# A transformer block with a product-key expert layer on one core: weights of v made for two chunks at a time, row dots written in place, h laid out in blocks of 32 tokens

## The chip, the cores and the metric

The kernel runs on one core of a Trainium2 chip. The metric is device time in microseconds of one execution of the whole program; lower is better. Engines are named as in the profile: PE (TensorE matmuls), PEld (its weight loads), DVE (VectorE), ACT (ScalarE), POOL (GpSimd), SP (SyncE, here a queue of DMA issues).

## What is computed

One block over 512 tokens of width 1024, in float32: adaptive norm, three kinds of attention, a projection, and a feed-forward layer of experts chosen by product keys. The change lies in the last part:

```python
def chunk(xc):                                   # xc: tokens x 1024
    q = einsum('td,de->te', xc, wq)              # 8 heads x 2 halves x 128
    s = einsum('thpd,hpnd->thpn', q, sub_keys)   # 128 key scores per half
    sv, si = top_k(s, 16)
    ...                                          # the best 16 of the 256 sums per head
    g = softmax(top)                             # gates of the 8 x 16 chosen experts
    a = gelu(einsum('thkd,td->thk', u[eidx], xc))
    return einsum('thk,thkd->td', g * a, v[eidx])
```

## The kernel before

The 16384 experts are 128 chunks of 128. Tokens 0 to 127 (tile 0) are done by gathering: for each of 128 choices two rows of 1024 per token are fetched by indirect DMA (from u and from v), a dot of the u row with h goes to a gelu, and the v row is added with that weight to `y0`. Tokens 128 to 511 are done densely: for each chunk all gelus are computed (`a_chunk`: u times h, 128 experts x 384 tokens) and multiplied by a table of gates that is zero for experts not chosen, and the result is the weight of a matmul with v (`v_chunk`).

Each float32 matmul is made of three passes on split operands: x_hi is x rounded to the matmul's type (ACT writes it), x_lo is the rest (DVE subtracts). So a chunk of u, of v, and of the weights w each need a hi and a lo, and h has both from the start (`h_hi`, `h_lo`, written once by `take_h2T` on ACT and `h_low` on DVE, from PSUM).

Stages, in order of time:

1. The mixer, to about 310 us.
2. Queries and key scores (`q_passes`, 24 matmuls for each of 16 pieces, moving operand h with all 512 tokens), to about 406 us.
3. Chunks 0 to 64 of `a_chunk`, 24 matmuls of 384 columns each, with the making of the gates table between them, to 768 us. Gelus of the first 56 chunks are stored to DRAM (`spill`).
4. The joint loop, to about 1290 us: step m does `v_chunk(m)` (18 matmuls of 512 columns) and then `a_chunk(m + 65)`.
5. v chunks alone, to about 1556 us; from m = 72 the gelus come back from DRAM, four chunks to a load (L1096), beside the gates (`g_in`, L1092).

Work is ordered by hand in each engine's program, with semaphores between engines. In step m of stages 4 and 5 DVE runs `chunk(m)`: `weigh(m)` (gelus times gates to `w_f`, a copy to `w_hi`, the rest to `w_lo`), `split_v(m)` (v_lo), one or two row dots with `row_sum`s, and u_lo for chunk m + 65. ACT runs `parts(m)`: v_hi of m + 1, the small gelus of the row dots, u_hi, and the gelu of `a_chunk(m + 64)`. `v_hi` and `v_lo` have two places, so ACT may write v_hi(m) only when `v_chunk(m - 2)` is done (semaphore `v_product_done`). `weigh` waits for that too, before its copy:

```python
dve.tensor_tensor(w_f..., a_act[:, c, :]..., g_in[:, (c // 4) % 2, :, c % 4, :], ALU.mult).then_inc(s_pw, 1)
dve.wait_ge(s_pw, i + 1)
if not end:
    after(dve, s_yv, i - 1)
dve.tensor_copy(hi[:, q, :], w_f[:, :]).then_inc(s_whi, 1)
dve.wait_ge(s_whi, i + 1)
dve.tensor_tensor(lo[:, q, :], w_f[:, :], hi[:, q, :].bitcast(f32), ALU.subtract)
```

`load_g` on SP loads gates (and from chunk 72 on gelus) of four chunks into one of two places, when the chunks that used the place are done. The last four chunks (`at_end`) have buffers of their own, so that PE can finish one output tile after the other.

## Time and profile before

| | us |
|---|---|
| device time, median of 3 runs | 1568.46 (1567.51 to 1569.08) |
| span of the profiled execution, first to last instruction | 1565.4 |
| PE busy (share of the span) | 1527.4 (98%) |
| DVE busy | 1337.7 (85%) |
| ACT busy | 660.1 (42%) |
| POOL busy | 487.5 (31%) |

The span leaves out what lies before the first and behind the last instruction, so it is 2.1 us under the lowest run and 3.1 us under the median. Matmuls overlap in the records: one is listed with some 0.39 us (512 columns), but the next begins 0.227 us after it. What a matmul costs is read from the distance between starts, and whether PE waits is read from gaps in that distance.

### The profile page before, as it was taken

The numbers are of one execution on the slowest core, as the hardware profiler recorded it, in microseconds if no ns is written. First come the engines' busy times: TensorE is split into PE (matmuls) and PEld (weight loads), VectorE is DVE, ScalarE is ACT, GpSimd is POOL, SyncE is SP. The second block draws the span as 40 slices with busy tenths as digits, with TensorE's granted clock in tenths as the row PEclk, the third lists the DMA queues.
The fourth block names the chain that finished last, engine by engine and source line by source line (L and its number), as shares of the span: only waits on it lengthen the run. The fifth ranks groups of instructions, "written<-read, shape, count | busy, mean of one in ns | idle before, by whom it ended". The sixth has DMA issues, their size and how long they took to land.

```text
span 1565.4 us, 24588 instructions
## 1 busy us (share of the span) xinstructions
PE 1527.4 (98%) x8275; PEld 1363.9 (87%) x8275; DVE 1337.7 (85%) x2877; ACT 660.1 (42%) x1143; POOL 487.5 (31%) x450
## 2 busy tenths in 40 slices
PE   4999999999999999999999999999999999999997
PEld 4887767888999999999999999999999998888886
DVE  5788666549999989899698898899999998999977
ACT  3444554233344757657433333343333332333232
POOL 1121300033450000020355455456566663233000
PEclk9999999999999999999999999999999999999999
DMA  9754410132355565676899999999999999999772
GB/s 366 270 174 148 148 68 0 55 95 82 118 169 180 194 230 199 229 248 251 298 393 330 350 340 343 346 337 371 372 378 372 368 345 355 376 350 352 241 244 104
DMA packets 160467, 398.77 MB, mean 255 GB/s; under 512 B 11753, under 2 KB 75369, under 8 KB 158705
## 3 DMA queue, kind: packets, MB, share of 16 engines
q1 hardware_dynamic: 112992, 227.06, 41.7%
q0 software_dynamic: 36864, 134.23, 23.2%
q10 hardware_dynamic: 10514, 36.30, 5.9%
q8 instruction: 47, 0.77, 0.2%
q14 instruction: 50, 0.41, 0.1%
HBM read 359.27 MB, written 38.27 MB: 254 GB/s over the span
## 4 chain that ended last, share of the span: by engine, by line
PE 83%; DVE 13%; DMA 1%; ACT 1%; issue 1%; ACTq 0%; DVEq 0%; SPq 0%
PE bank_S L907 16%; PE bank_T L907 11%; PE bank_O L858 6%; PE bank_O L856 6%; PE bank_O L857 6%; PE bank_T L885 5%; PE bank_G L907 5%; PE bank_S L856 3%; PE bank_S L857 3%; PE bank_S L858 3%; PE bank_O L643 2%; PE bank_S L610 2%; DVE mod_acc L1909 1%; DVE v_sb L1902 1%; DVE v_sb L1915 1%; DVE si L1921 1%
## 5 line engine op out<-in xcount | busy, mean ns | idle before, releaser
L1462 ACT ACTIVATE v_hi<-v_raw 128x1024 fp32r<-128x1024 f32 x124 | 131.7, 1062 | 333.9 <-PE bank_G L907 330.9
L1434 ACT ACTIVATE u_hi<-u_raw 128x1024 fp32r<-128x1024 f32 x128 | 135.9, 1061 | 243.0 <-PE bank_O L858 122.8
L1213 POOL COPY stage<-eidx 128x1 uint32<-128x1 uint32 (+1 forms) x128 | 75.7, 591 | 461.8 <-DVE eidx L2030 207.7
L1217 POOL DMA_INDIRECT row<-in_peer_u,stage x128 | 148.1, 1157 | 103.8 <-POOL stage L1213 103.8
L856 PE MATMUL bank_S<-h_hi,u_hi 128*128 128x384 f32 x512 | 179.7, 351 | 0.5 <-DVE u_lo L2002 0.5
L858 PE MATMUL bank_O<-h_hi,u_lo 128*128 128x384 f32 x512 | 171.9, 336 | 0.0
L856 PE MATMUL bank_O<-h_hi,u_hi 128*128 128x384 f32 x512 | 171.7, 335 | 0.0
L858 PE MATMUL bank_S<-h_hi,u_lo 128*128 128x384 f32 x512 | 171.5, 335 | 0.0
L857 PE MATMUL bank_O<-h_lo,u_hi 128*128 128x384 f32 x512 | 171.5, 335 | 0.0
L857 PE MATMUL bank_S<-h_lo,u_hi 128*128 128x384 f32 x512 | 171.4, 335 | 0.0
L2098 DVE SCALAR_TENSOR_TENSOR y<-row,wgt,y 128x1024 f32<-128x1024 f32 x128 | 165.9, 1296 | 0.0
L2108 DVE TENSOR_TENSOR v_lo<-v_raw,v_hi 128x1024 fp32r<-128x1024 f32 x124 | 152.0, 1226 | 12.1 <-ACT v_hi L1462 0.6
L2121 DVE SCALAR_TENSOR_TENSOR junk<-row,h 128x1024 f32<-128x1024 f32 x128 | 155.8, 1217 | 0.0
L1217 POOL DMA_INDIRECT row<-in_peer_v,stage x128 | 141.6, 1106 | 41.9 <-issue 30.3
L907 PE MATMUL bank_S<-v_hi,w_lo 128*128 128x512 f32 x372 | 125.4, 391 | 0.0
L907 PE MATMUL bank_S<-v_lo,w_hi 128*128 128x512 f32 x372 | 125.3, 391 | 0.0
L907 PE MATMUL bank_S<-v_hi,w_hi 128*128 128x512 f32 x372 | 125.2, 391 | 0.0
L1505 ACT ACTIVATE g_out<-bank_T 128x512 f32<-128x512 f32 x96 | 104.7, 1122 | 46.6 <-PE bank_T L885 38.2
L2057 DVE TENSOR_SCALAR hot_i<-iota_k,cols 128x128 f32<-128x128 f32 x384 | 106.6, 341 | 1.0 <-PE bank_T L885 0.2
L885 PE MATMUL bank_T<-hot_i,hot_j 128*128 128x128 f32 x768 | 101.8, 275 | 1.2 <-DVE hot_j L2059 1.2
L885 PEld LDWEIGHTS bank_T<-hot_i,hot_j 128*128 128x128 f32 x768 | 97.6, 191 | 3.6 <-issue 2.1
L856 PEld LDWEIGHTS bank_O<-h_hi,u_hi 128*128 128x128 f32 x512 | 96.1, 188 | 2.5
(370 smaller groups left out, 3647.8 us busy)
## 6 DMA issues: line engine op xcount, KB each, us to landing
u_raw<-in_u_t SPq DMA_DIRECT2D x128, 512.0 KB
v_raw<-in_peer_v SPq DMA_DIRECT2D x128, 512.0 KB
gates<-g_out ACTq DMA_DIRECT2D x12, 2048.0 KB, 6.8
g_in<-gates SPq DMA_DIRECT2D x32, 768.0 KB
ada_late<-in_w_ada SPq DMA_DIRECT2D x8, 2048.0 KB, 8.4
spill<-a_act ACTq DMA_DIRECT2D x56, 192.0 KB, 2.1
a_act<-spill SPq DMA_DIRECT2D x14, 768.0 KB, 10.6
w_raw<-in_w_in SPq DMA_DIRECT2D x20, 512.0 KB, 4.1
```

Of the source, the lines that this page charges most:

```text
L856: pe.matmul(ps[:, 0:DT], u_hi[q][:, kk], h_hi[:, GT:NT, k, :], start=(k == 0), stop=False)
L857: pe.matmul(ps[:, 0:DT], u_hi[q][:, kk], h_lo[:, GT:NT, k, :], start=False, stop=False)
L858: mm = pe.matmul(ps[:, 0:DT], u_lo[q][:, kk], h_hi[:, GT:NT, k, :], start=False, stop=(k == KD - 1))
L885: mm = pe.matmul(ps[:, tok * P:tok * P + P], hot_j[:, b % 2, tok, :], hot_i[:, b % 2, tok, :], start=True, stop=True)
L907: mm = pe.matmul(y_bank[t][half][:, :], w[:, q, tt], v[:, q, half * 512:half * 512 + 512], start=(first and n == 0), stop=False)
L1217: pool.indirect_dma_start(rows[slot][:, :], None, table[:, :], bass.IndirectOffsetOnAxis(stage[:, place:place + 1], 0))\
L1434: act.activation(u_hi[c % 2][:, :], u_raw[:, c % 2, :], ACT.Copy).then_inc(s_uhi, 1)
L1462: act.activation(v_hi_end[:, i % TAIL, :] if end else v_hi[:, c % 2, :], v_raw[c % 4][:, :], ACT.Copy)\
L2057: dve.tensor_scalar(hot_i[:, B % 2, tok, :], iota_k[:, :], cols[:, 0, n:n + 1], cols[:, 2, n:n + 1], ALU.is_equal, ALU.mult)
L2098: dve.scalar_tensor_tensor(out=y0[:, :], in0=rows[2 * place + 1][:, :], scalar=wgt[:, q], in1=y0[:, :], op0=ALU.mult, op1=ALU.add).then_in ...
L2108: dve.tensor_tensor(lo[:, q, :], v_raw[c % 4][:, :], hi[:, q, :].bitcast(f32), ALU.subtract)\
L2121: dve.scalar_tensor_tensor(out=junk[:, :], in0=rows[2 * place][:, :], scalar=1.0, in1=h2[:, 0, :], op0=ALU.mult, op1=ALU.mult, accum_out=d ...
```

## The change

- **Weights in pairs.** `weigh` is gone. On DVE `product` multiplies gelus by gates for two chunks in one instruction and writes the result over the gates in `g_in`; ACT's new `w_high` makes w_hi of both chunks; DVE's `w_low` makes w_lo of both. In step m, DVE does `w_low` of the pair (m, m + 1) if m is even and `product` of the pair (m + 1, m + 2) if m is odd, in front of `split_v(m)`. ACT does `w_high` of the pair (m + 2, m + 3) at the end of `parts(m)`, m even. `w_hi` and `w_lo` have two places of a pair each. PE waits for the pair's count.
- **Loads of gates** now wait for w_lo of the pairs that used the place, where they waited for the products.
- **Row dots** write their full-length product over the gathered u row, where they wrote to `junk`.
- **h in blocks.** `h_hi` and `h_lo` are stored as 16 blocks of 32 tokens (block, then the 8 pieces of the width, then the token), where there were 4 tiles of 128. The moving operand of each matmul of `a_chunk` is then 12 runs of 32 columns, 256 values (1024 bytes) apart, where it was 3 runs of 128; in `q_passes` 16 runs instead of 4.
- **Places.** Several buffers move in memory; `u_lo1` now lies over tile 0 of `h_lo`, for which POOL waits once for the last query.

```diff
-        h_hi = at("h_hi", 32, [P, NT, KD, P], f32r)
-        h_lo = at("h_lo", 64, [P, NT, KD, P], f32r)
+        h_hi = at("h_hi", 32, [P, S // GB, KD, GB], f32r)
+        h_lo = at("h_lo", 64, [P, S // GB, KD, GB], f32r)
...
+        def gate_pair(c):
+
+            return g_in[c // 4 % 2][:, :, c % 4:c % 4 + 2, :].rearrange("p b i t -> p i b t")
+
+        def by_block(pair):
+            return pair.rearrange("p i (b t) -> p i b t", t=GB)
...
-                    pe.matmul(ps[:, 0:DT], u_hi[q][:, kk], h_hi[:, GT:NT, k, :], start=(k == 0), stop=False)
+                    pe.matmul(ps[:, 0:DT], u_hi[q][:, kk], h_hi[:, GT * P // GB:S // GB, k, :], start=(k == 0), stop=False)
...
-                pe.wait_ge(s_w, i + 1)
+                pe.wait_ge(s_w, over(i, c, 2) + 1)
                 pe.wait_ge(s_vlo, i + 1)
...
-                    after(sp, s_pw, 4 * (q - 1))
+                    after(sp, s_w, 2 * (q - 1))
...
+                if i == 1:
+                    taken(pool, ("q", 2 * PH - 1))
...
-                act.activation(h_hi[:, i, 4 * half:4 * half + 4, :], ps, ACT.Copy).then_inc(s_hhi, 1)
+                act.activation(half_columns(h_hi, i, half), ps.rearrange("p a (n t) -> p a n t", t=GB), ACT.Copy)                   .then_inc(s_hhi, 1)
...
+            def w_high(i, c):
+
+                if not within(i):
+                    return
+                if at_end(i):
+                    act.wait_ge(s_acc, PH * TOPK)
+                else:
+                    after(act, s_yv, i - 2)
+                act.wait_ge(s_pw, over(i, c, 2) + 1)
+                act.activation(weight_pair(w_hi, w_hi_end, i, c), gate_pair(c), ACT.Copy).then_inc(s_whi, 1)
...
             act.wait_ge(s_gst[1], 16 * (BLOCKS // 2))
+            w_high(0, 0)
+
...
+                if c % 2 == 0:
+                    w_high(m + 2, c + 2)
...
+            def product(i, c):
+
+                if not within(i):
+                    return
+                late = isinstance(i, int) and i >= MAIN
+                dve.wait_ge(s_g[c // 4 % 2], 16 * (over(i, c, 8) + 1))
                 if late:
-                    dve.wait_ge(s_al[c // 4], 2 * (i - c) - 2 * MAIN + 16)
+                    dve.wait_ge(s_al[c // 4 % 2], 16 * ((i - MAIN) // AHEAD + 1))
                 else:
-                    dve.wait_ge(s_gelu, i + SPILL + 1)
...
+                    dve.wait_ge(s_gelu, i + SPILL + 2)
+                slot = c % AHEAD
+                dve.tensor_tensor(gate_pair(c), by_block(a_act[:, slot:slot + 2, :]), gate_pair(c), ALU.mult)\
+                   .then_inc(s_pw, 1)
+
+            def w_low(i, c):
+
+                dve.wait_ge(s_whi, over(i, c, 2) + 1)
+                if not at_end(i):
+                    after(dve, s_yv, i - 2)
+                dve.tensor_tensor(weight_pair(w_lo, w_lo_end, i, c), gate_pair(c),
+                                  weight_pair(w_hi, w_hi_end, i, c).bitcast(f32), ALU.subtract).then_inc(s_w, 1)
...
-                weigh(i, c, late)
+                if c % 2 == 0:
+                    w_low(i, c)
+                else:
+                    product(i + 1, c + 1)
...
-                    dve.scalar_tensor_tensor(out=junk[:, :], in0=rows[2 * place][:, :], scalar=1.0, in1=h2[:, 0, :],
+                    dve.scalar_tensor_tensor(out=rows[2 * place][:, :], in0=rows[2 * place][:, :], scalar=1.0,
+                                             in1=h2[:, 0, :],
...
+            product(0, 0)
             chunk_loop(dve, chunk_and_tile)
```

DVE at the entry of the joint loop, before: v_lo of chunk 0, then the three instructions of `weigh(0)`, the first row dot, u_lo of chunk 65, `weigh(1)` and v_lo of chunk 1.

```order
L2108 TENSOR_TENSOR v_lo<-v_raw_132,v_hi 128x1024 [waits gates_stored0,v_hi_ready,gates_made,vector_steps]
L2076 TENSOR_TENSOR w_f<-a_act,g_in 128x384 [waits gelu_done,gates_loaded0,gates_stored1]
L2085 CAST w_hi<-w_f 128x384 [waits w_product]
L2087 TENSOR_TENSOR w_lo<-w_f,w_hi 128x384 [waits w_hi]
L2121 SCALAR_TENSOR_TENSOR junk,dots<-row_150,h_107 128x1024 [waits row_got0,w_ready]
L2131 TENSOR_TENSOR u_lo_140<-u_raw,u_hi_138 128x1024 [waits u_hi_ready]
```

The same place with the change: the product (`g_in<-a_act,g_in`) and w_lo of the pair, between which DVE waits for ACT (`waits w_hi`), and in step 1 the product of the next pair in front of v_lo of chunk 1.

```order
L2142 TENSOR_TENSOR v_lo<-v_raw_133,v_hi 128x1024 [waits gates_stored0,v_hi_ready,gates_made,vector_steps]
L2114 TENSOR_TENSOR g_in_130<-a_act,g_in_130 128x2x12x32 [waits gelu_done,gates_loaded0,gates_stored1]
L2122 TENSOR_TENSOR w_lo_150<-g_in_130,w_hi_148 128x768 [waits w_hi]
L2158 SCALAR_TENSOR_TENSOR row_152,dots<-row_152,h_107 128x1024 [waits row_got0]
L2169 TENSOR_TENSOR u_lo_141<-u_raw,u_hi_139 128x1024 [waits u_hi_ready]
L2114 TENSOR_TENSOR g_in_130<-a_act,g_in_130 128x2x12x32 [waits gelu_done,gates_loaded0]
L2142 TENSOR_TENSOR v_lo<-v_raw_134,v_hi 128x1024 [waits v_hi_ready]
```

What moved: the making of w_hi has left DVE, and the first v chunk now waits for a chain over DVE, ACT and DVE again. ACT at the same place with the change, from v_hi of chunk 0 to v_hi of chunk 2:

```order
L1482 ACTIVATE v_hi<-v_raw_133 128x1024 [waits v_loaded0,gates_stored0]
L1454 ACTIVATE u_hi_139<-u_raw 128x1024 [waits u_loaded1,a_done]
L1502 ACTIVATE a_act<-bank_S 128x384 [waits a_done,gelus_stored1]
L1494 ACTIVATE w_hi_148<-g_in_130 128x768 [waits w_product,gates_stored1]
L1482 ACTIVATE v_hi<-v_raw_134 128x1024 [waits v_loaded1]
L1562 ACTIVATE act_g<-dots 128x1 [waits row_dots]
L1565 ACTIVATE wgt<-act_g,gate 128x1 [waits row_gelus]
L1454 ACTIVATE u_hi_138<-u_raw 128x1024 [waits u_loaded0,a_done]
L1502 ACTIVATE a_act<-bank_O 128x384 [waits a_done,w_product]
L1494 ACTIVATE w_hi_149<-g_in_130 128x768 [waits w_product]
L1482 ACTIVATE v_hi<-v_raw_135 128x1024 [waits v_loaded2,v_product_done]
```

The two `w_hi` rows are new; v_hi of chunks 1 and 2 now stand behind them. DVE in stage 5, steps 118 to 120, before:

```order
L2108 TENSOR_TENSOR v_lo<-v_raw_134,v_hi 128x1024 [waits v_hi_ready,w_ready]
L2141 TENSOR_SCALAR ss<-ss 128x1 [waits x2_squares]
L2076 TENSOR_TENSOR w_f<-a_act,g_in 128x384 [waits gelus_loaded1,gates_loaded1]
L2085 CAST w_hi<-w_f 128x384 [waits v_product_done,w_product]
L2087 TENSOR_TENSOR w_lo<-w_f,w_hi 128x384 [waits w_hi]
L2108 TENSOR_TENSOR v_lo<-v_raw_135,v_hi 128x1024 [waits v_hi_ready,w_ready]
L2076 TENSOR_TENSOR w_f<-a_act,g_in 128x384 [waits gelus_loaded0,gates_loaded0]
```

And with the change:

```order
L2142 TENSOR_TENSOR v_lo<-v_raw_135,v_hi 128x1024 [waits v_hi_ready]
L2179 TENSOR_SCALAR ss<-ss 128x1 [waits x2_squares]
L2114 TENSOR_TENSOR g_in_130<-a_act,g_in_130 128x2x12x32 [waits gelus_loaded0,gates_loaded0]
L2142 TENSOR_TENSOR v_lo<-v_raw_136,v_hi 128x1024 [waits v_hi_ready]
L2122 TENSOR_TENSOR w_lo_150<-g_in_130,w_hi_148 128x768 [waits v_product_done,w_hi]
L2142 TENSOR_TENSOR v_lo<-v_raw_133,v_hi 128x1024 [waits v_hi_ready]
```

The instruction that waits for the loads of chunks 120 to 123 (`gelus_loaded0`, `gates_loaded0`) stood behind v_lo of chunk 119 and now stands in front of it.

## Rows read from the trace of the kernel before

**Rows 1.** The page: busy time of the engines, and the chain that ended last.

```profile
PE 1527.4 (98%) x8275; PEld 1363.9 (87%) x8275; DVE 1337.7 (85%) x2877; ACT 660.1 (42%) x1143; POOL 487.5 (31%) x450
...
PE 83%; DVE 13%; DMA 1%; ACT 1%; issue 1%; ACTq 0%; DVEq 0%; SPq 0%
```

**Rows 2.** Windows: PE, PEld, DVE, ACT, POOL busy (count), granted clock, DMA share, GB/s.

```profile
1080.00:1120.00 40.00, 40.00 (x205) 36.44 (x204) 38.23 (x51) 15.54 (x33) 25.34 (x26) 1.00 0.99 364
...
1360.00:1400.00 40.00, 40.00 (x178) 33.15 (x177) 37.00 (x56) 12.56 (x20) 12.36 (x15) 1.00 1.01 358
```

**Rows 3.** Timeline of PE in the joint loop: start, duration, what; two steps' first matmuls.

```profile
792.82 0.63 PE L907 MATMUL bank_S<-v_hi,w_hi 128*128 128x512 f32 x2
...
801.12 0.63 PE L907 MATMUL bank_S<-v_hi,w_hi 128*128 128x512 f32 x2
```

**Rows 4.** Timeline of PE: 18 matmuls of `q_passes`, and one v chunk of stage 5.

```profile
330.90 0.39 PE L811 MATMUL bank_S<-h_hi,wq_hi 128*128 128x512 f32 x1
...
334.98 0.60 PE L797 MATMUL bank_T<-keys,qT 128*128 128x128 f32 x4
...
1515.65 0.62 PE L907 MATMUL bank_S<-v_hi,w_hi 128*128 128x512 f32 x2
...
1519.73 0.62 PE L907 MATMUL bank_S<-v_hi,w_hi 128*128 128x512 f32 x2
```

**Rows 5.** Timeline of PE: the last a chunk of stage 3, and the first v chunk.

```profile
763.74 0.33 PE L856 MATMUL bank_O<-h_hi,u_hi 128*128 128x384 f32 x1
...
767.89 0.63 PE L907 MATMUL bank_S<-v_hi,w_hi 128*128 128x512 f32 x2
```

**Rows 6.** Groups by line and form: count, busy us, mean ns, idle before and its releasers.

```profile
L2098 DVE SCALAR_TENSOR_TENSOR y<-row,wgt,y 128x1024 f32<-128x1024 f32 x128 | 165.9, 1296 | 0.0
L2108 DVE TENSOR_TENSOR v_lo<-v_raw,v_hi 128x1024 fp32r<-128x1024 f32 x124 | 152.0, 1226 | 12.1 <-ACT v_hi L1462 0.6 <-DVE w_lo L2087 0.3
...
L1434 ACT ACTIVATE u_hi<-u_raw 128x1024 fp32r<-128x1024 f32 x128 | 135.9, 1061 | 243.0 <-PE bank_O L858 122.8 <-PE bank_S L858 79.3 <-DMA u_raw<-in_u_t 18.2
...
L1505 ACT ACTIVATE g_out<-bank_T 128x512 f32<-128x512 f32 x96 | 104.7, 1122 | 46.6 <-PE bank_T L885 38.2 <-ACT a_act L1471 8.4
...
L2076 DVE TENSOR_TENSOR w_f<-a_act,g_in 128x384 f32<-128x384 f32 x128 | 70.4, 550 | 1.1 <-ACT a_act L1471 1.0
L2087 DVE TENSOR_TENSOR w_lo<-w_f,w_hi 128x384 fp32r<-128x384 f32 x124 | 69.4, 559 | 4.3
...
L2085 DVE CAST w_hi<-w_f 128x384 fp32r<-128x384 f32 x124 | 45.2, 365 | 47.5 <-PE bank_G L907 40.4 <-DVE w_f L2076 0.4
...
L1471 ACT ACTIVATE a_act<-bank_O 128x384 f32<-128x384 f32 x64 | 30.3, 474 | 4.7 <-PE bank_O L858 4.7
```

**Rows 7.** Waits: who waited for whom, us in total, times, longest.

```profile
ACT v_hi L1462 <- PE bank_G L907: 330.9, 121, 3.6
```

**Rows 8.** Timeline at the entry of the joint loop, POOL and DVE.

```profile
765.42 0.18 POOL L1213 COPY stage<-eidx 128x1 uint32<-128x1 uint32 x1 [70.47 <-DMA g_in<-gates]
...
765.45 0.57 DVE L2076 TENSOR_TENSOR w_f<-a_act,g_in 128x384 f32<-128x384 f32 x1 [1.02 <-ACT a_act L1471]
...
766.44 0.56 DVE L2087 TENSOR_TENSOR w_lo<-w_f,w_hi 128x384 fp32r<-128x384 f32 x1
```

**Rows 9.** Loads of gelus from DRAM (L1096), one of their issues, and v_lo of chunk 119.

```profile
DMA to landing us min/median/max: 7.9/10.6/12.0
...
1502.80 0.75 SPq L1096 DMA_DIRECT2D a_act<-spill  x1
...
1517.02 1.23 DVE L2108 TENSOR_TENSOR v_lo<-v_raw,v_hi 128x1024 fp32r<-128x1024 f32 x1
```

**Rows 10.** Timelines of DVE and PE: where h_lo and the last v_lo are ready and used.

```profile
313.67 0.69 DVE L1800 TENSOR_TENSOR h_lo<-bank_T,h_hi 128x512 fp32r<-128x512 f32 x1 [0.29 <-ACT h_hi L1360]
...
316.72 0.47 PE L811 MATMUL bank_S<-h_hi,wq_hi 128*128 128x512 f32 x1
...
1544.22 1.23 DVE L2108 TENSOR_TENSOR v_lo_end<-v_raw,v_hi_end 128x1024 fp32r<-128x1024 f32 x1
...
1546.93 0.39 PE L916 MATMUL bank_S<-v_hi_end,w_hi_end 128*128 128x512 f32 x1
```

68 lines of the change are left out of this document (29 added, 39 removed).

## The prediction

> **What bounds the kernel now.** I read the page first, for who is busy and whose work ends last: PE is busy 98% of the span and 83% of the last-ending chain is PE; DVE has 13% of it [rows 1]. A busy PE in this profile is not yet a PE without gaps, since records overlap, so the second view is the windows of the stages that the change touches. In the joint loop PE is busy all of 40 us, DVE 38.23 of 40; in the v stage PE all of 40, DVE 37.00. The granted clock is 1.00 in both, its 2.4 GHz level, and the DMA engines are full, 0.99 and 1.01 [rows 2]. Third, distances between starts, to see whether PE waits anywhere. A step of the joint loop takes 801.12 - 792.82 = 8.30 us [rows 3]. Alone, its parts take 767.89 - 763.74 = 4.15 us (24 matmuls of 384 columns) [rows 5] and 1519.73 - 1515.65 = 4.08 us (18 of 512) [rows 4], 8.23 in sum. So at most 0.07 us of a step is anything but matmuls, and nothing can be won there but those 63 x 0.07 = 4.4 us. Fourth, the waits: ACT waits 330.9 us for the end of v chunks, 121 times, before it may write the next v_hi [rows 7]. That is the signature of a bound PE: the makers of operands are early and are held back by PE's use of the buffers. The reader should keep two questions apart: how much DVE work goes away (much), and whether PE ever waited for it (no).
>
> **Part 1, weights in pairs: the work.** A DVE subtraction takes 1226 ns for 1024 elements and 559 for 384 [rows 6], 1.04 ns an element, so 768 take 559 + 384 x 1.04 = 0.96 us. Before, a pair of chunks cost 2 x (0.550 + 0.365 + 0.559) = 2.95 us on DVE; with the change 0.96 (product) + 0.96 (w_low) = 1.92. DVE loses 1.03 us a pair, 66 us over 64 pairs. The product reads gates in runs of 32 already in `w_f` (0.550 us, no dearer than w_lo's 0.559), so the pair's pattern adds nothing. ACT gains 64 copies of 768: between its copies of 384 (0.474) and 1024 (1.061) lies 0.83 us [rows 6]; 53 us in all on an engine busy for 660 [rows 1]. All of it is hidden, because PE does not wait for DVE or ACT in either loop. Worth on the end: 0. If DVE had been what PE waits for, 66 us would be at stake; the 0.07 us of a step say that it isn't.
>
> **Part 2, the entry of the loop: the one place with a price.** Before, the gates land at 765.42 (POOL is released by them), DVE's `w_f` starts at 765.45, and w_lo is ready at 766.44 + 0.56 = 767.00 [rows 8]; PE ends its last a chunk at 767.89 and goes on without a gap [rows 5]. Slack 0.89 us. Now the product ends at 765.45 + 0.96 = 766.41, w_high at 766.46 + 0.83 = 767.29, w_low at 767.34 + 0.96 = 768.30 (0.05 us for each passing from engine to engine, the order of the 0.03 us between landing and `w_f` in these rows). PE starts `v_chunk(0)` at 768.35: **+0.45 us**. By the bounds of w_high (0.80, proportional to u_hi's 1061 ns, to 1.06, all of it) it is 0.4 to 0.7. Behind the wait on ACT stands v_hi of chunk 1, now done at 768.4; its v_lo is needed 8.3 us after the loop's start. On DVE the first dot and u_lo of chunk 65 stand behind w_low: ready at 768.3 + 1.3 + 1.2 = 770.8 (by the instructions of their length in [rows 6]), needed at 768.35 + 4.1 = 772.4. Nothing further is late.
>
> **Part 3, inside the loops.** ACT's w_high(m + 2) waits for the product that DVE makes at the start of step m + 1, and v_hi(m + 2) stands behind it. But v_hi(m + 2) waits for `v_chunk(m)` anyway, and DVE, tied to v_hi(m + 1), is in step m + 1 before that. Cost 0. On DVE the product of chunks 4q and 4q + 1 now stands ahead of v_lo(4q - 1), and it waits for loads. Take chunk 120: its gelus are issued at 1502.80; the product could start after v_lo(118), about 1514.1 (one 4.08 step before the end of v_lo(119), 1518.2); the slowest of the 14 loads took 12.0 us, landing at 1514.8; v_lo(119) starts at 1517.02 in any case, held by PE [rows 9]. PE needs v_lo(119) at 1519.73 [rows 4], so it stays unharmed up to a landing at 1519.73 - 1.23 - 0.96 - 0.1 = 1517.4, 14.6 us after the issue. Margin 2.6 us over the worst. Cost 0.
>
> **Part 4, the tail, the dots, the new wait of POOL.** The last v_lo is ready at 1544.22 + 1.23 = 1545.45 and used at 1546.93 [rows 10]; DVE is lighter there than before, so it is not later. Cost 0. The dot writes to another address; if in place it took what the dearest instruction of its length takes, 1.296 us [rows 6], 128 of them still fit into DVE's slack and what it just lost. POOL's new wait is for the last query, which ACT's u_hi(1), already awaited, stands behind. Cost 0.
>
> **Part 5, h in blocks.** The evictions: 8 copies by ACT and 8 subtractions by DVE, now written in runs of 32. No row has a write in such runs by ACT; its nearest are contiguous ones (0.59 for 512, between 0.474 and 1.061) and `g_out`'s, scattered by single elements, 1.122 [rows 6]. Runs of 32 are nearer to contiguous: 0. The upper bound, +0.53 twice behind the last tile, would still meet 316.72 - 314.36 = 2.4 us of slack at the first matmul that reads it [rows 10]; it could hold up the other copies there by 0.5 us. The matmuls: 1 run (v, 512 columns) and 4 runs (`q_passes`, 512 columns, 334.98 - 330.90 = 4.08 us for 18) cost the same, 226.7 ns each [rows 4], and 3 runs cost 4.15/24 = 172.9 [rows 5]. Taking columns off at 2.4 GHz leaves 13.3, 13.3 and 12.9 ns. Runs therefore cost nothing that can be seen: at the 0.01 us of these rows, under 0.2 ns for each run more. I take 0. Upper bound: 9 runs more x 0.2 x 3120 matmuls (24 in each of 128 chunks, and 48 of the first queries, on three tiles) plus 12 x 0.2 x 336 (the other 14 queries) = 6.4 us. Below zero is excluded, since one run is no cheaper than four.
>
> Beside these rows, the Trainium skill (TensorE: Matmul & The Clock Gate, on 56 ns instead of 53.3) states a fixed cost of some 2.5 ns per warm matmul over N / 2.4 GHz. The rows differ, 13 ns, and they decide. If the 10.5 ns between were the price of how the moving operand is read, new runs could change 3120 matmuls by up to 33 us, an estimate from that page; that the contiguous v pays the same speaks against it. And SBUF — State Buffer (on cachelines) says that reads are at full rate while hits on a 16-byte line are consecutive, which runs of 32 floats keep: by that rule the block form costs 0 as well, where the bound above is 6.4; no row here has PE reading runs this short.
>
> **The sum.** On the profiled execution's own time, span 1565.4: +0.45 = 1565.85 us. The median of the runs is 3.1 us over that span; so **1568.9 us**, in effect no change. A change under 0.2% (3.1 us) can't be told from none by such runs.
>
> **Rivals.**
> 1. *Short runs slow the matmuls* (slower). If each run more costs one cycle of the 2.4 GHz clock, 0.42 ns, it is 9 x 0.42 x 3120 + 12 x 0.42 x 336 = 13.5 us: 1582.4. It decides from 0.9 ns a matmul on (3.1 us / 3456). For it: no row has such runs. Against it: 1, 3 and 4 runs cost alike. Chance 0.12.
> 2. *DVE waits for loads ahead of v_lo* in the v stage (slower). Each of 14 loads would pay what it lands later than 14.6 us after its issue; 1 us each makes 1582.9. Against it: the slowest took 12.0. With other small losses, chance 0.05.
> 3. *The 0.07 us of a step come from DVE and ACT beside PE*, and a lighter DVE gives them back (faster): up to 4.4 us, 1564.5. Against it: ACT gets more to do at just these moments. Chance 0.09.
> 4. *DVE or its buffers hold PE somewhere that I don't see*, so that part of the 66 us is real (faster); 5 to 10 us, some 1561. Against it: the steps' arithmetic. Chance 0.06.
> 5. *The pairing saves DVE nothing*, since the long patterns run slower: then DVE is as busy as now, and PE still doesn't wait: 1568.9, in with the forecast.
>
> **The numbers.** Forecast with rival 5: 0.68, its own range 1566 to 1572. Faster 0.15 (3 and 4), slower 0.17 (1 and 2). The range takes in most of rival 3, the upper bound of 6.4 us and half of rival 1: 1563.5 to 1576. Left out: the far ends of 1, 2 and 4, some 0.14.
>
> **What the profile after should show.** A step of the joint loop still 8.30 us, a v chunk 4.08, both to 0.01; a matmul of 384 columns in stage 3 at 173 ns and `q_passes` at 226.7 (rival 1: 176 to 177 and more). DVE busy near 1272, ACT near 713. The first v chunk at about 768.3, with a gap of 0.45 us before it. The product 0.96 us, w_high 0.83. v_hi still waiting for PE some 300 us. Any distance of v chunks over 4.08 in the v stage, once in four, is rival 2; a step under 8.27 is rival 3. I would be wrong above all if the distance of matmuls depends on the layout of h.

## The result: 11 us slower

| | before | with the change |
|---|---|---|
| device time, median | 1568.77 us (1567.51 to 1570.10, 4 runs) | 1580.07 us (1579.26 to 1580.31, 4 runs) |
| span of the profiled execution | 1565.4 us | 1578.5 us |

The ratio is 1.0073, with a 95% interval of 1.0059 to 1.0087. The forecast was 1568.9 us with a range up to 1576. The time lies above that range, on the side of rival 1. The medians are 11.3 us apart. The two profiled executions, from which all that follows is read, are the fastest of the four before and the slowest of the four after, 12.8 us apart and 13.1 in span; a sum by stages therefore comes out somewhat above 11.3.

The page of the changed kernel, busy times and the chain that ended last, against [rows 1]:

```profile
PE 1541.2 (98%) x8275; PEld 1377.0 (87%) x8275; DVE 1273.5 (81%) x2621; ACT 706.3 (45%) x1207; POOL 544.1 (34%) x450
...
PE 95%; DVE 3%; DMA 1%; ACT 1%; issue 0%; SPq 0%; DVEq 0%; ACTq 0%
```

DVE is lighter by 64.2 us and ACT heavier by 46.2, near what was forecast. But PE, with the same 8275 matmuls, is busy for 13.8 us more, and the span is 13.1 longer. An engine that does the same instructions in more busy time has not waited: its instructions have become slower.

Windows in the joint loop and in the v stage (columns as in [rows 2]):

```profile
1090.00:1130.00 40.00, 40.00 (x204) 36.69 (x203) 35.64 (x40) 17.20 (x35) 27.20 (x26) 1.00 0.99 369
1370.00:1410.00 40.00, 40.00 (x178) 33.11 (x178) 31.93 (x36) 16.01 (x25) 19.28 (x16) 1.00 1.00 352
```

The granted clock is 1.00, the 2.4 GHz level, as before, so the clock is not the reason. Next the distances. PE's timeline, the starts of two steps of the joint loop, against [rows 3]:

```profile
793.93 0.63 PE L924 MATMUL bank_S<-v_hi,w_hi 128*128 128x512 f32 x2
...
802.30 0.63 PE L924 MATMUL bank_S<-v_hi,w_hi 128*128 128x512 f32 x2
```

A step takes 8.37 us; it took 8.30. The same timeline in `q_passes` (18 matmuls from the first row to the second) and, behind them, one v chunk of stage 5, against [rows 4]:

```profile
331.00 0.40 PE L829 MATMUL bank_S<-h_lo,wq_hi 128*128 128x512 f32 x1
...
335.26 0.40 PE L829 MATMUL bank_S<-h_lo,wq_hi 128*128 128x512 f32 x1
...
1520.56 0.62 PE L924 MATMUL bank_S<-v_hi,w_hi 128*128 128x512 f32 x2
...
1524.64 0.62 PE L924 MATMUL bank_S<-v_hi,w_hi 128*128 128x512 f32 x2
```

The v chunk still takes 4.08 us, although its weights are now made in pairs. 18 matmuls of the queries, which the pairs don't touch, take 4.26 instead of 4.08. The third place is the last a chunk of stage 3 and the first v chunk, against [rows 5]:

```profile
772.67 0.34 PE L873 MATMUL bank_O<-h_hi,u_hi 128*128 128x384 f32 x1
...
776.76 0.34 PE L875 MATMUL bank_O<-h_hi,u_lo 128*128 128x384 f32 x1
777.11 0.70 PE L924 MATMUL bank_S<-v_hi,w_hi 128*128 128x512 f32 x2
```

Here the last matmul starts 4.09 us after the chunk's first, 23 distances of 178 ns, and then 0.35 us pass instead of 0.18: a gap of 0.17. The groups by form say the same of all chunks. The row of before, of one of the three passes of an a chunk:

```profile
L857 PE MATMUL bank_O<-h_lo,u_hi 128*128 128x384 f32 x512 | 171.5, 335 | 0.0
```

and of the changed kernel:

```profile
L874 PE MATMUL bank_O<-h_lo,u_hi 128*128 128x384 f32 x512 | 174.1, 340 | 0.0
```

PE does not stand idle in front of either ("0.0" in both rows). The whole loss, by stage, from the starts of all matmuls in the two traces:

| | before | with the change | difference |
|---|---|---|---|
| up to the first query | 302.52 | 303.14 | +0.62 |
| queries, to the first a chunk | 104.04 | 107.37 | +3.33 |
| stage 3, to the first v chunk | 361.33 | 366.59 | +5.26 |
| joint loop | 523.14 | 527.02 | +3.88 |
| v alone | 265.19 | 265.17 | -0.02 |
| mean distance, queries (512 columns) | 230.9 ns | 240.2 ns | +9.3 |
| mean distance, a chunks of stage 3 (384) | 173.4 ns | 177.8 ns | +4.4 |

The distances of the queries are those of the steady part, and those of stage 3 of its first 80 us. The mean of a query includes its first distance, 314 ns before and 321 with the change; most of the others are 227 before and 233 to 240 now. The loss sits wherever PE reads h, and nowhere else. Summed over every matmul of a kind, the distances close the account: queries +3.32 us (384 matmuls), a chunks of stage 3 +5.63 (1560, on average +3.6 ns, since later in the stage some were dearer already), the gates' matmuls among them -0.37, a chunks of the joint loop +4.83 (1511 distances, +3.2 ns), v chunks of the joint loop -0.95 (1134). That is 12.46 us, the three stages' 12.47. The rest of the 13.1 is the 0.62 ahead of the first query, which lies in front of everything changed.

The rest of the changed kernel's profile. Groups by form of what was new or moved:

```profile
L2142 DVE TENSOR_TENSOR v_lo<-v_raw,v_hi 128x1024 fp32r<-128x1024 f32 x124 | 151.9, 1225 | 119.0 <-ACT v_hi L1482 118.9
...
L2114 DVE TENSOR_TENSOR g_in<-a_act,g_in 128x768 f32<-128x768 f32 x64 | 60.9, 951 | 2.6 <-DMA a_act<-spill 1.9 <-DMA g_in<-gates 0.7
...
L2122 DVE TENSOR_TENSOR w_lo<-g_in,w_hi 128x768 fp32r<-128x768 f32 x62 | 58.9, 951 | 1.0 <-ACT w_hi L1494 1.0
...
L1494 ACT ACTIVATE w_hi<-g_in 128x768 fp32r<-128x768 f32 x62 | 51.7, 834 | 1.9 <-DVE g_in L2114 1.9
```

The waits of the pair that makes v's parts, the first against [rows 7]:

```profile
ACT v_hi L1482 <- PE bank_G L924: 286.8, 122, 3.6
...
DVE v_lo L2142 <- ACT v_hi L1482: 118.9, 116, 5.1
```

v_lo now stands idle for v_hi 118.9 us in all (0.6 in [rows 6]), and v_hi stands idle for PE. Not all of this is new: before, DVE waited for PE in front of its copy to w_hi (47.5 us of idle time in [rows 6]), and that wait has moved to v_lo. Over the whole span DVE's idle time, span less busy time, grew from 227.7 to 305.0 us: 64.2 of freed work and 13.1 of longer span. So the saving became idle time and went no further.

### The profile page after: what moved, and what is told of

Its sections match the earlier page's. It is cut to its first block, busy times and chain, and to the rows that moved or that the text cites. A ratio compares the mean times of both kernels' runs of the same rounds, so it can differ in the third digit from the quotient of the medians.

```text
span 1578.5 us, 24179 instructions
## 1 busy us (share of the span) xinstructions
PE 1541.2 (98%) x8275; PEld 1377.0 (87%) x8275; DVE 1273.5 (81%) x2621; ACT 706.3 (45%) x1207; POOL 544.1 (34%) x450
## 4 chain that ended last, share of the span: by engine, by line
PE 95%; DVE 3%; DMA 1%; ACT 1%; issue 0%; SPq 0%; DVEq 0%; ACTq 0%
PE bank_S L924 16%; PE bank_T L924 11%; PE bank_O L873 6%; PE bank_O L875 6%; PE bank_O L874 6%; PE bank_S L873 6%; PE bank_S L875 6%; PE bank_S L874 6%; PE bank_T L902 5%; PE bank_G L924 5%; PE bank_S L830 2%; PE bank_S L828 2%; PE bank_S L829 2%; PE bank_O L659 2%; PE bank_S L626 2%; PE bank_T L639 1%
## 5 line engine op out<-in xcount | busy, mean ns | idle before, releaser
L2142 DVE TENSOR_TENSOR v_lo<-v_raw,v_hi 128x1024 fp32r<-128x1024 f32 x124 | 151.9, 1225 | 119.0 <-ACT v_hi L1482 118.9
L1233 POOL COPY stage<-eidx 128x1 uint32<-128x1 uint32 (+1 forms) x128 | 98.8, 772 | 414.1 <-DVE eidx L2064 209.9
L1237 POOL DMA_INDIRECT row<-in_peer_u,stage x128 | 159.0, 1242 | 104.1 <-POOL stage L1233 103.0
L873 PE MATMUL bank_S<-h_hi,u_hi 128*128 128x384 f32 x512 | 183.0, 357 | 0.0
L1237 POOL DMA_INDIRECT row<-in_peer_v,stage x128 | 164.5, 1285 | 41.9 <-issue 41.3
L875 PE MATMUL bank_S<-h_hi,u_lo 128*128 128x384 f32 x512 | 174.8, 341 | 0.0
L875 PE MATMUL bank_O<-h_hi,u_lo 128*128 128x384 f32 x512 | 174.4, 341 | 0.0
L2158 DVE SCALAR_TENSOR_TENSOR row<-row,h 128x1024 f32<-128x1024 f32 x128 | 156.6, 1224 | 0.0
L874 PEld LDWEIGHTS bank_O<-h_lo,u_hi 128*128 128x128 f32 x512 | 96.5, 188 | 2.5
```

The source lines that it names most:

```text
L873: pe.matmul(ps[:, 0:DT], u_hi[q][:, kk], h_hi[:, GT * P // GB:S // GB, k, :], start=(k == 0), stop=False)
L874: pe.matmul(ps[:, 0:DT], u_hi[q][:, kk], h_lo[:, GT * P // GB:S // GB, k, :], start=False, stop=False)
L875: mm = pe.matmul(ps[:, 0:DT], u_lo[q][:, kk], h_hi[:, GT * P // GB:S // GB, k, :], start=False, stop=(k == KD - 1))
L1237: pool.indirect_dma_start(rows[slot][:, :], None, table[:, :], bass.IndirectOffsetOnAxis(stage[:, place:place + 1], 0))\
L2142: dve.tensor_tensor(lo[:, q, :], v_raw[c % 4][:, :], hi[:, q, :].bitcast(f32), ALU.subtract)\
L2158: dve.scalar_tensor_tensor(out=rows[2 * place][:, :], in0=rows[2 * place][:, :], scalar=1.0, in1=h2[:, 0, :], op0=ALU.mult, op1=ALU.mult, ...
```

## The experiments

### First: undo the block form, or do it alone

`e1_pairs_tiles128` is the changed kernel with h in tiles of 128 again:

```diff
-        h_hi = at("h_hi", 32, [P, S // GB, KD, GB], f32r)
-        h_lo = at("h_lo", 64, [P, S // GB, KD, GB], f32r)
+        h_hi = at("h_hi", 32, [P, S // HB, KD, HB], f32r)      # HB = 128
+        h_lo = at("h_lo", 64, [P, S // HB, KD, HB], f32r)
```

> The changed kernel with h stored again in 4 tiles of 128 tokens; pairs, dots in place and all places in memory stay as changed. Theory R (the price is the short runs of the moving operand): the median falls back to that of the kernel before plus the entry gap of the joint loop, less what the changed kernel won in its joint loop (v matmuls there 228.2 ns against 229.1): 1566 to 1569 us, a matmul of 384 columns at 173 ns and of q_passes at 227 to 231 in the mean. Rival P (the pairs or the new places, u_lo over the old h_lo tile, cost it): it stays at 1578 to 1580 with 177 to 178 ns.

Measured: 1569.03 us (11 runs) against 1568.11, ratio 1.0006 (0.9997 to 1.0015). Its distances are those of before: queries 230.8, a chunks 173.4 ns.

`e2_before_blocks32` is the kernel before with that one edit the other way, h in blocks of 32 (HB = 32), and nothing of pairs, dots or places:

> The kernel before with h alone in blocks of 32 tokens, nothing else changed. Theory R: 11 to 15 us over the kernel before (q_passes +3.2 us, the other a matmuls 3072 x 4.4 ns = 13.5 us), 1580 to 1584 us; a matmul of 384 columns at 177 to 178 ns. Rival P: no change, 1568 to 1569 us, 173 ns.

Measured: 1579.82 us (5 runs), ratio 1.0075 (1.0061 to 1.0089). Queries 107.37 us, stage 3 366.70, joint loop 526.92, v alone 265.17, distances 240.2 and 177.8 ns: each the number of the changed kernel. PE's line on its page, 12.6 us more busy than before's, though DVE (1342.4) is as heavy as before:

```profile
PE 1540.0 (98%) x8275; PEld 1375.5 (87%) x8275; DVE 1342.4 (85%) x2877; ACT 659.3 (42%) x1143; POOL 479.3 (30%) x450
```

Undone, the edit takes the loss away; alone, it brings all of it. That settles which part of the change was slow. What it is in a block of 32 that costs is another question.

`e3_before_blocks64` is the same with HB = 64:

> The kernel before with h alone in blocks of 64 tokens (6 runs of 64 for a chunk, 8 for a query). Theory R with a price for each run (about 0.5 ns): +1.5 ns a matmul, 4 to 6 us over the kernel before, 1573 to 1575 us. Rival T (a threshold: runs of 64 or more are free, shorter ones are not): 1568 to 1569 us, 173 ns. Rival T2 (any jump beyond one in 128 columns costs all of it): as with blocks of 32, 1580 us or more.

Measured: 1567.79 us (10 runs), ratio 0.9998 (0.9988 to 1.0007); distances 230.8 and 173.4 ns. Twice the runs of before cost nothing that can be seen, four times the runs cost 11.7 us. A price for each run, theory R, does not give that.

`e4_forms` is the kernel before; its first 64 a chunks read 384 columns of h in six ways in turn (other columns than the right ones in all but the 3 runs of 128, so other numbers are computed):

```diff
+                form = FORMS[i % len(FORMS)] if early else 3      # FORMS = (1, 3, 6, 12, 24, 40)
...
+                    elif form == 12:
+                        pe.matmul(ps[:, 0:DT], u_hi[q][:, kk], h_flat[:, :].rearrange("p (n a t) -> p n a t", n=12, a=KD)[:, :, k, :], start=(k == 0), stop=False)
...
+                    elif form == 40:
+                        pe.matmul(ps[:, 0:DT], u_hi[q][:, kk], h_flat[:, 360 * k:360 * k + 480].rearrange("p (n t) -> p n t", t=40)[:, :, 0:32], start=(k == 0), stop=False)
```

> The kernel before, but the first 64 a chunks read their 384 moving columns in six forms in turn, from the same 12 KB of h: 1 run of 384, 3 of 128 (as before), 6 of 64, 12 of 32, 24 of 16 (all with the spacing that fills the region), and 12 runs of 32 spaced 160 bytes instead of 1024. But for the form of 3 the columns are not those of the right tokens and width, so the gelus of these chunks are of other numbers. Distances between matmuls: theory R, linear in the runs: 172.5, 173.4, 175, 178, 184 ns, and the close spacing like the wide one, 178. Rival T: 173, 173, 173, 178, 178 or more. Rival S (the spacing of 1024 bytes, a power of two, is what costs): 12 runs of 160 bytes spacing at 173, others by their spacing.

Its groups by line in stage 3; the lines are the third pass of 6 runs of 64 (L867), 12 of 32 at 1024 bytes (L871), 24 of 16 at 512 (L875) and 12 of 32 at 160 (L879):

```profile
L867 PE MATMUL bank_S<-h_hi,u_lo 128*128 128x384 f32 x88 | 29.5, 335 | 0.0
...
L871 PE MATMUL bank_S<-h_hi,u_lo 128*128 128x384 f32 x84 | 28.7, 341 | 0.0
...
L875 PE MATMUL bank_S<-h_hi,u_lo 128*128 128x384 f32 x80 | 27.4, 343 | 0.0
...
L879 PE MATMUL bank_S<-h_hi,u_lo 128*128 128x384 f32 x80 | 26.9, 337 | 0.0
```

Median distances: one run of 384 columns 174, 3 and 6 runs 173, 12 runs at 1024 bytes 178, 24 runs 181, but 12 runs at 160 bytes 174. The same number of runs of the same length is dear or cheap by where the runs lie. R and the threshold at a length, T, fell here; the spacing, S, was left, and a new one, C.

### Second: spacing and length, and the pairs once more

The next kernels use one frame: nine forms take the first 64 a chunks in turn, each on lines of its own. A form is given by the columns in a run, the values of 4 bytes from run to run, and a third number. In the two kernels of this part the third is how many values the start moves from one piece k of the width to the next; in the two of the third part it is the first value, the same for all k, and the forms count from the start of tile 0 instead of tile 1. The first form is always h as in the kernel before.

```diff
+FORMS = [(128, 0, 0), (32, 40, 320), (32, 64, 320), (32, 96, 256), (32, 128, 192), (32, 192, 96), (32, 248, 8), (32, 250, 8), (32, 256, 0)]
...
+                    h, l = (spaced(x, k, *FORMS[form]) for x in (h_hi, h_lo))
```

> The kernel before. Of the first 64 chunks of u times h, each of nine forms of the moving operand takes every ninth: 3 runs of 128 as before, then 12 runs of 32 columns with the starts of the runs 160, 256, 384, 512, 768, 992, 1000 and 1024 bytes apart (the columns are not the right ones in these eight forms, so other numbers are computed there; 384 columns are multiplied in each). What is read is the distance between the starts of two matmuls, by form. Known so far: 3 runs of 128 173 ns, 12 of 32 at 160 bytes 174, at 1024 bytes 177 to 179. Theory C (a jump costs PE reading time, more for a far jump, and about 13 ns of each matmul, its distance less 384 columns at 2.4 GHz, cover it): the distance rises smoothly with the spacing, 173 to 174 up to 256 bytes, about 175 to 176 at 512 and 768 bytes, 177 to 178 at 992, 1000 and 1024 alike. Theory S (spacing by a power of two is what costs): 1024 bytes 177 to 178, 512 bytes perhaps too, and 992, 1000, 768 and 384 near 173 to 174. Theory T (the length of the run decides, whatever the spacing): all eight at 177 to 178 but 160 bytes, which would be the odd one; it has nearly fallen already.

> The kernel before. Of the first 64 chunks of u times h, each of nine forms of the moving operand takes every ninth: 3 runs of 128 as before, then 4 runs of 96 (3072 bytes apart), 6 of 64 (2048), 8 of 48 (1536), 16 of 24 (768), 16 of 24 (128 bytes apart), 24 of 16 (512), 24 of 16 (96 bytes apart), 48 of 8 (256); the columns are the right ones but in the two close forms, 16 of 24 at 128 bytes and 24 of 16 at 96, and all multiply 384. Read: distance between starts. Theory C (n jumps of about 1.45 ns of reading, less for a near jump, are hidden up to about 13 ns a matmul): 4, 6 and 8 runs 173 ns, 16 runs of 24 about 180 to 183, 24 of 16 at 512 bytes 181 to 182 (known), the close forms only 174 to 177, and 48 of 8 over 190. Theory R' (each run over three costs, in proportion): 4 runs 173.5, 6 runs 175, 8 runs 176, 16 runs 180: 6 and 8 runs tell it from C. Theory T (a run under 64 columns costs a fixed sum a matmul): 8 of 48 stands at 177 to 178 already, with 16 of 24 beside it.

One thing in the second text is wrong: in all its forms but the first the columns are not the right ones. All multiply 384 all the same. These two ran once, as did `e4_forms` and the two kernels of the third part, and only their distances are used.

The third pass in the first of the two, spacings of 1000 bytes (L899), 512 (L887), 256 (L879), 160 (L875), 384 (L883) and 992 (L895):

```profile
L899 PE MATMUL bank_S<-h_hi,u_lo 128*128 128x384 f32 x56 | 19.7, 352 | 0.0
...
L887 PE MATMUL bank_S<-h_hi,u_lo 128*128 128x384 f32 x56 | 19.2, 343 | 0.0
...
L879 PE MATMUL bank_S<-h_hi,u_lo 128*128 128x384 f32 x56 | 19.2, 342 | 0.0
...
L875 PE MATMUL bank_S<-h_hi,u_lo 128*128 128x384 f32 x56 | 18.8, 336 | 0.0
...
L883 PE MATMUL bank_S<-h_hi,u_lo 128*128 128x384 f32 x56 | 18.8, 335 | 0.0
...
L895 PE MATMUL bank_S<-h_hi,u_lo 128*128 128x384 f32 x56 | 18.8, 335 | 0.0
```

And in the second, 4 runs of 96 (L875), 6 of 64 (L879), 48 of 8 (L903) and 16 of 24 at 128 bytes (L891):

```profile
L875 PE MATMUL bank_S<-h_hi,u_lo 128*128 128x384 f32 x56 | 19.1, 342 | 0.0
...
L879 PE MATMUL bank_S<-h_hi,u_lo 128*128 128x384 f32 x56 | 18.8, 336 | 0.0
L903 PE MATMUL bank_S<-h_hi,u_lo 128*128 128x384 f32 x50 | 18.8, 376 | 0.0
...
L891 PE MATMUL bank_S<-h_hi,u_lo 128*128 128x384 f32 x56 | 18.7, 334 | 0.0
```

How to read a duration here: 335 goes with a distance of 173 to 174 ns, 342 with 180; the rest of the duration overlaps the next matmul. All median distances stand in the table below. C fell: 256 bytes are dearer than 384, 4 runs of 96 dearer than 6 of 64 and than 16 of 24. S fell too, since 768 bytes cost and so do 96s at 3072, and neither is a power of two. A price for each run over three (R') fell by the 96s at 180, where it had 173.5, and a price for every run under 64 columns (T) by the 96s and by the 16 runs of 24 at 173.

`e7_after_blocks64` is the changed kernel with HB = 64, the question whether anything of the pairs' part is worth having:

> The changed kernel whole, but with h in 8 blocks of 64 tokens, so that a matmul of 384 columns reads 6 runs of 64 and one of 512 columns 8. Theory C (6 and 8 runs are hidden): 384-column matmuls at 173.4 ns, the queries' at 230.9, and the time of the kernel before within 0.2%: 1567.5 to 1570.5 us, against 1580 with blocks of 32. If blocks of 32 lose in proportion to the number of runs, 64 would lose about a third of it, 4 us: 1572. What is left to the pairs of weights is then seen alone: the gap of about half a microsecond at the entry of the joint loop, 0 to +1 us in all. A gain of over 0.2% over before would speak for the pairs freeing something, which the tiles of 128 did not show.

Measured: 1569.48 us (11 runs) against 1568.33, ratio 1.0009 (1.0000 to 1.0018), distances 230.9 and 173.4 ns. It confirms blocks of 64 as free in a second kernel, and with `e1_pairs_tiles128` it bounds the pairs, the dots and the places together: about 1 us slower, and no gain.

### Third: what makes a run dear

One spacing of 32s that was cheap stood out: 384 bytes are 3 x 128, an odd number, while 256, 512, 768, 1024 and, for the 96s, 3072 are even ones. Theory B was made from that. Cut each row of SBUF into pieces of 128 bytes, 32 columns, and call them even and odd in turn; dear is a matmul in which a piece is followed by one of the same kind.

```diff
-FORMS = [(128, 0, 0), (32, 40, 320), ...
+FORMS = [(128, 0, 0), (32, 224, 0), (32, 288, 0), (32, 320, 0), (96, 800, 0), (64, 544, 0), (128, 1056, 0), (24, 160, 0), (16, 160, 0)]
```

> Theory C has fallen by the two kernels before this: 4 runs of 96 at 3072 bytes took 180 ns, dearer than 6 runs of 64; 12 runs of 32 at 384 bytes took 174, but at 256 bytes 180. New theory B: SBUF hands PE 128 bytes (32 columns) at a time from two sides, told apart by the start address over 128, even or odd; a matmul goes at its best, 173.4 ns for 384 columns, if such pieces come from the even and the odd side in turn, and loses up to 7 ns if a piece is followed by one of the same side, as with starts 256, 512, 768 or 1024 bytes apart. Nine forms in the first 64 chunks, all with 384 columns (other columns than the right ones but in the first form): 3 runs of 128; 12 of 32 at 896, 1152 and 1280 bytes; 4 of 96 at 3200; 6 of 64 at 2176; 3 of 128 at 4224; 16 of 24 at 640; 24 of 16 at 640. B: 896 and 1152 (odd multiples of 128) 173 to 174, 1280 (even) 179 to 180; 96 at 3200 174 where 3072 took 180; 64 at 2176 178 to 180 where 2048 took 174, since now the end of a run and the next start are of one side; 128 at 4224 over 175; 24 at 640 173 to 174 where 768 took 176. Rival D (distance from start to start or the number of runs alone, in some form that smaller tests missed): 896, 1152 and 1280 alike near 178, 96 at 3200 like 3072 at 180, 64 at 2176 and 128 at 4224 unchanged at 174. Rival S (multiples of 256 for any length): 64 at 2176 and 128 at 4224 would be the fastest, 173.

The third pass at 896, 1152 and 1280 bytes (L878, L882, L886), 96s at 3200 (L890) and 64s at 2176 (L894):

```profile
L886 PE MATMUL bank_S<-h_hi,u_lo 128*128 128x384 f32 x56 | 19.2, 343 | 0.0
...
L894 PE MATMUL bank_S<-h_hi,u_lo 128*128 128x384 f32 x56 | 19.0, 340 | 0.0
...
L878 PE MATMUL bank_S<-h_hi,u_lo 128*128 128x384 f32 x56 | 18.8, 335 | 0.0
L882 PE MATMUL bank_S<-h_hi,u_lo 128*128 128x384 f32 x56 | 18.8, 335 | 0.0
...
L890 PE MATMUL bank_S<-h_hi,u_lo 128*128 128x384 f32 x56 | 18.8, 335 | 0.0
```

| form of 384 columns | spacing, bytes | of 128 | median distance, ns |
|---|---|---|---|
| 3 of 128 | 4096 | 32 | 173 to 174 |
| 3 of 128 | 4224 | 33 | 173 |
| 6 of 64 | 2048 | 16 | 174 |
| 6 of 64 | 2176 | 17 | 177 |
| 4 of 96 | 3072 | 24 | 180 |
| 4 of 96 | 3200 | 25 | 174 |
| 12 of 32 | 384, 896, 1152 | 3, 7, 9 | 174, 174, 174 |
| 12 of 32 | 256, 512, 1280 | 2, 4, 10 | 180, 180, 180 |
| 12 of 32 | 768, 1024 | 6, 8 | 178, 178 to 180 |
| 12 of 32 | 160, 992, 1000 | no multiple | 174, 173, 188 |
| 8 of 48 | 1536 | 12 | 177 |
| 16 of 24 | 768; 640; 128 | 6; 5; 1 | 175; 174; 173 |
| 24 of 16 | 512; 640; 96 | 4; 5; no multiple | 181 to 183; 180; 178 |
| 48 of 8 | 256 | 2 | 209 |

What B said ahead of the run: 896 and 1152 cheap and 1280 dear, as measured; 96s cured by the odd spacing and 64s harmed by it, as measured (the 64s 1 ns less than said). This is the sharpest pair, since neither a rule of even spacings nor one of run counts can give opposite signs. 24s at 640 at 174, as said. One statement failed: 128s at 4224 bytes were called dear and are not; if B is right, two repeats inside a matmul are hidden.

The spread between 178 and 180 has an order that the table hides. The forms of 32 that stand at 180 (256, 512 and 1280 bytes, and 1024 in `e5_spacing_of_32`) begin on an even piece for every k. Those at 177 to 179 (768 bytes, and 1024 in `e4_forms`, in the changed kernel and in `e2_before_blocks32`) begin on even and odd pieces in turn from k to k. So what a matmul takes depends a little on its neighbours too.

`e9_shifted_starts` moves the beginnings:

```diff
+FORMS = [(128, 0, 0), (64, 512, 32), (64, 512, 16), (128, 1024, 32), (128, 1024, 16), (384, 384, 16), (96, 768, 32), (32, 96, 16), (32, 256, 16)]
```

> The same frame, forms with shifted starts (other columns than the right ones but in the first form): 3 runs of 128; 6 of 64 at 2048 bytes begun at byte 128 and at byte 64; 3 of 128 at 4096 begun at 128 and at 64; one run of 384 begun at 64; 4 of 96 at 3072 begun at 128; 12 of 32 at 384 and at 1024 begun at 64. Theory B: begun at 128 nothing changes against the start at 0 (64s 174, 128s 173, 96s 180), because only the change of side counts; one run of 384 begun at 64 stays at 173 to 175; 64 and 128 begun at 64 touch a piece of 128 bytes twice by halves at each jump, so 175 to 178; 32 at 1024 begun at 64 reads both sides in each run, half and half, and is the open one: 174 if a half piece is as good as a whole, up to 185 if each half takes the time of a whole. Rival A (what counts is that a run starts on a multiple of its own length or of 256 bytes): 64s begun at 128 would be slow, 96s begun at 128 change too.

Measured, median distances: 64s begun at byte 128 175 and at byte 64 173; 128s 175 and 173; one run of 384 begun at 64 173; 96s begun at 128 176; 32s at 384 bytes begun at 64 173, at 1024 bytes begun at 64 177. This is a mixed answer. One run of 384 stays cheap, as B has it, but a start at 128, which by B changes nothing, costs 64s and 128s 1 to 2 ns and takes 4 from the 96s, and halves of pieces (begun at 64) were cheaper than expected in both lengths. For the 64s and 128s begun at 128 the median hides a pattern: behind the first few matmuls of a chunk every fifth takes 181 to 182 ns, the others 173 to 177. Nothing in B has a period of five. Rival A, that a run has to start on a multiple of its length, fares no better: 64s begun at 64 are at their best. So B orders the spacings of whole pieces as long as the starts are not shifted; the effect of the start is not explained.

### Fourth: whole kernels with runs of 32

If B is right, all 128 chunks can read 12 runs of 32 at no cost, if these lie an odd number of pieces apart. Two kernels, the kernel before with one function between, and one number different (other columns than the right ones in both):

```diff
+STEP, KSTEP = 224, 32          # the second kernel: 256, 32
...
+            def spaced(x, k):
+                flat = x[:, GT:NT, :, :].rearrange("p t k c -> p (t k c)")[:, 0:12 * STEP]
+                return flat.rearrange("p (n t) -> p n t", t=STEP)[:, :, KSTEP * (k % 7):KSTEP * (k % 7) + 32]
...
-                    pe.matmul(ps[:, 0:DT], u_hi[q][:, kk], h_hi[:, GT:NT, k, :], start=(k == 0), stop=False)
+                    pe.matmul(ps[:, 0:DT], u_hi[q][:, kk], spaced(h_hi, k), start=(k == 0), stop=False)
```

> The kernel before, whole, with h as before; every one of the 128 chunks of u times h reads 12 runs of 32 columns whose starts lie 896 bytes apart, 7 x 128 (not the right columns, so other numbers; 384 are multiplied). The queries are as before. Theory B (what costs is a piece of 128 bytes followed by one from the same side, even or odd): with 12 runs in every matmul nothing is lost, distance 173 to 174 ns, stage 3 361.3 us, joint loop 523.1, the whole at the time of before within 0.2%, 1567 to 1571 us. Rival R (12 runs cost, however they lie, and the small tests were lucky in their surroundings): as with 1024 bytes, 1576 to 1577.

> The same kernel with one number changed: the starts lie 1024 bytes apart, 8 x 128, as in blocks of 32 tokens; other columns than the right ones again. Both theories: distance 177 to 179 ns, stage 3 366.6 us, joint loop 526.9, and a total of that of the kernel with blocks of 32 in its h alone (1579.8) less the 3.3 us that the queries lost there: 1576 to 1577 us. Together with the kernel at 896 bytes it tells B from R in whole time: 8 us between the two by B, 0 by R.

| | 896 bytes | 1024 bytes |
|---|---|---|
| device time, median | 1570.37 us (10 runs) | 1578.13 us (4 runs) |
| ratio to before (1568.24) | 1.0014 (1.0005 to 1.0024) | 1.0069 (1.0052 to 1.0086) |
| stage 3, joint loop | 363.71, 523.57 us | 367.02, 527.76 us |
| mean distance in stage 3 | 175.2 ns | 178.3 ns |

The third pass in stage 3, first of the kernel at 896 bytes:

```profile
L863 PE MATMUL bank_S<-h_hi,u_lo 128*128 128x384 f32 x504 | 169.5, 336 | 0.0
```

and of the kernel at 1024:

```profile
L863 PE MATMUL bank_S<-h_hi,u_lo 128*128 128x384 f32 x499 | 170.5, 342 | 0.0
```

One number in the address of the runs is worth 7.8 us, where B said 8 and R 0. The kernel at 1024 bytes lies 1.1 us above its 1576 to 1577. The one at 896 is inside its 1567 to 1571, but its distance (175.2 ns for 173 to 174) and its stage 3 (363.71 us for 361.3) are not what B said, and it is 2.1 us slower than the kernel before, where B said that nothing is lost. The distances say where: taken by the place in the chunk, all stand at 173 to 175 ns except the first matmuls of pieces k = 1, 3 and 5, at 180 to 182, and the one behind each of these, at 176. There the matmul ahead ends on an odd piece and this one begins on an odd one, a repeat between two matmuls instead of within one, which was not in the expectation. But at k = 2, 4 and 6 an even piece follows an even one in the same way, at 174 to 175 ns. So half of these repeats cost, and B doesn't say why the other half don't.

## Why the prediction was wrong, point by point

- **What bounds the kernel** was read rightly: PE, and PE alone. What PE's matmuls gained went into the time: +13.8 us busy, +13.1 of span. The reading "at most 0.07 us of a step is anything but matmuls" was right too. It says that waits can't matter; it doesn't say that matmuls can't. (The 172.9 ns for 3 runs come from one chunk; the mean is 173.4.)
- **Part 1, the pairs' work.** The product takes 0.95 us (0.96 forecast), w_low 0.95 (0.96), w_high 0.83 (0.83). DVE lost 64.2 us (66), ACT gained 46.2 (53). Worth on the end 0, as `e1_pairs_tiles128` shows: 1.0006.
- **Part 2, the entry.** In the changed kernel the timelines of POOL, DVE and ACT show, against [rows 8]:

```profile
773.92 0.18 POOL L1233 COPY stage<-eidx 128x1 uint32<-128x1 uint32 x1 [72.71 <-DMA g_in<-gates]
...
773.95 0.97 DVE L2114 TENSOR_TENSOR g_in<-a_act,g_in 128x768 f32<-128x768 f32 x1 [0.70 <-DMA g_in<-gates]
...
775.01 0.85 ACT L1494 ACTIVATE w_hi<-g_in 128x768 fp32r<-128x768 f32 x1 [0.70 <-DVE g_in L2114]
...
775.89 0.96 DVE L2122 TENSOR_TENSOR w_lo<-g_in,w_hi 128x768 fp32r<-128x768 f32 x1 [0.97 <-ACT w_hi L1494]
```

  The chain is the one forecast, and takes 777.11 - 773.95 = 3.16 us where 2.90 was worked out. PE's last chunk ended later here, since its matmuls were slower, and so only 0.17 us of gap was left. The unhidden price shows in `e1_pairs_tiles128`, in the timelines of DVE and PE:

```profile
765.10 0.97 DVE L2115 TENSOR_TENSOR g_in<-a_act,g_in 128x768 f32<-128x768 f32 x1 [0.89 <-DMA g_in<-gates]
...
767.04 0.96 DVE L2123 TENSOR_TENSOR w_lo<-g_in,w_hi 128x768 fp32r<-128x768 f32 x1 [0.97 <-ACT w_hi L1495]
...
767.51 0.34 PE L876 MATMUL bank_O<-h_hi,u_lo 128*128 128x384 f32 x1
768.26 0.70 PE L925 MATMUL bank_S<-v_hi,w_hi 128*128 128x512 f32 x2 [0.41 <-DVE w_lo L2123]
```

  768.26 - 767.51 - 0.17 = 0.58 us, against +0.45 and its bounds 0.4 to 0.7. What was sized too small is the passing from DVE to PE: w_lo ends at 768.00 and PE starts 0.26 later, not 0.05.
- **Part 3, the loads.** The v stage kept its length, 265.17 us, so no load was late for PE. It was nearer than forecast. The loads of gelus and the wait of the product for them, in the changed kernel:

```profile
  DVE g_in L2114: 1.9, 2
...
DMA to landing us min/median/max: 8.0/11.2/14.1
```

  The slowest took 14.1 us where 14.6 was the limit worked out, and DVE did wait 1.9 us for them. The margin of 2.6 us over the worst of one trace was 0.5 in the next.
- **Part 4, the tail, the dots in place, POOL's wait:** no cost to be seen; a dot takes 1224 ns in place.
- **Part 5, h in blocks: the step that failed.** The term for the matmuls was put at 0, with 6.4 us as its upper bound; it measured 12.5 us over the three stages. "Runs therefore cost nothing that can be seen ... under 0.2 ns for each run more." That was drawn from forms of 1, 3 and 4 runs, each at least 128 columns long, with pieces in alternating order, and carried to 12 and 16 runs. Measured: 4.4 ns for a matmul of 384 columns and 9.3 for one of 512, above the bounds of 1.8 and 2.4. By the prediction's own counts that would be 3120 x 4.4 + 336 x 9.3 = 16.9 us; the stages show 12.5, because a chunks whose matmuls were already dearer (next to v or gates matmuls) lose less, 3.2 to 3.6 ns on average, and their neighbours give 1.3 us back. The fault is in the logic: a row that shows equal costs bounds the cost of what it holds, not of what is outside it. The last sentence of the prediction's expectations named the right danger.
- **Rival 1** was what happened, with a chance of 0.12 given to it, and its sign for the a chunks, 176 to 177 ns and more, was seen at 177.8. Its pricing was not right: cost does not go by the run. `e3_before_blocks64` has 6 runs at no cost, and `e10_all_32_at_896` 12 at about 2 us in the whole kernel. That its 13.5 us come near the measured 11.3 is luck.
- **Rivals 2, 3 and 4** did not occur. For 3 and 4, `e1_pairs_tiles128` is the test: DVE lighter by 68 us, the joint loop 523.22 against 523.14. So the 0.07 us of a step are not DVE's; ACT, heavier by 46.7 us in that kernel, was made lighter in no run. The distances before show where they lie: the 18 of a v chunk sum to 4.12 us in the joint loop and 4.08 alone, and the first six of an a chunk behind it take 171 to 185 ns. The cause is open.
- **The cachelines.** At 1000 bytes from run to run a matmul takes 188 ns, at 992 bytes 173, and at 1024 up to 180. The Trainium skill (SBUF — State Buffer, on cachelines) has reads at full rate while hits on a 16-byte line are consecutive. The first pair agrees in direction: at 1000 bytes every second run begins in the middle of such a line. The third doesn't: its runs keep to whole lines, and by the rule the block form would have cost 0.

What is shown: the block form is all of the loss; neither the number of runs nor their length alone decides; leaving aside the shifted starts of `e9_shifted_starts`, spacings of an odd number of 128-byte pieces are cheap and even ones dear for runs of 32 and of 96, and the reverse, more weakly, for 64. That order of pieces is a rule that fits these forms; that SBUF serves them from two sides is not shown. What stays open: why a piece after one of its own kind costs, how much each costs (3 repeats and the one to the next matmul cost 96s as much as 11 cost 32s), which repeats between matmuls count, the effect of the start, and runs of 16 and 8 columns, which lie up to 10 and 36 ns over the 173 of 3 runs, the 16s hardly less at an odd spacing. A rival for the mechanism was not tried either: a weight load runs beside each matmul, and no run changed where the weights lie, so the dear pieces may collide with its reads and not with each other. A whole kernel with right numbers and its blocks padded to 1152 bytes was not tried; the places on both sides of h are taken. No version found here beats the kernel before: the best, tiles of 128 or blocks of 64, with pairs or without, lie within 0.1% of it.

## What to carry to other kernels

- When PE is the bound, the address pattern of the moving operand is a cost like its columns. For a 4-byte operand of 384 columns the forms without cost here were runs of 64 or 128 columns at even multiples of 128 bytes, begun at an even one; runs of 32 at odd multiples were nearly so. Here that decided over 11 us, with nothing in the waits to show it.
- Where a trace's rows show that something is free, ask how far they reach. Four runs said nothing of twelve, and one small kernel with six forms would have said it.
- Work taken from an engine that is not waited for shows up as that engine's idle time (DVE's 64.2 us here), and the end does not move.

## What the hardware did that I had not expected

A matmul of 384 fp32 columns takes 174 ns if it reads 12 runs of 32 spaced by 384, 896 or 1152 bytes, and 180 if these are spaced by 256, 512 or 1280 and every matmul begins on an even piece. The same shift of spacing by 128 bytes turns 96s from 180 to 174 and 64s from 174 to 177. The effect also passes from one matmul to the next (180 to 182 instead of 174 at three places of a chunk in the kernel at 896 bytes). The pattern of distances is so steady that the median for a place in the chunk is the same to 1 ns over 38 chunks in the changed kernel and in the kernel with blocks of 32 alone.
